# Two product blocks of the first weight tile inside the prologue of a one-core hybrid layer kernel

## What is computed

```python
h = rmsnorm(x, norm_mix_g)
proj = h @ w_in            # w_in: 1024 x 9232, f32
q, k, v, gate_a = slices of proj, 64 columns per head
k, v                       # also outputs (new_k, new_v)
```

## Time and profile before

| | |
|---|---|
| median of 3 runs | 2689.96 us (2687.56 to 2692.24) |
| span of the profiled execution | 2689.6 us |
| PE busy | 2613.3 us, 97% of the span |
| DVE, ACT, POOL busy | 1493.0, 876.8, 345.1 us |
| DMA moved | 214.21 MB, 80 GB/s on average |
| first 40th of the span (67 us) | PE busy 6 tenths, PE clock 8 tenths |
| every other 40th | PE busy 9 tenths but in three of them (7, 8, 7) |

### The profile page before, as it was taken

How to read it: one execution, slowest core, us unless ns; L and a number is a source line. 1 busy time by engine, 2 the same in 40 slices (tenths; PEclk the granted TensorE clock), 3 DMA queues, 4 the chain that set the end, 5 groups by cost and what they waited for, 6 DMA issues and landing times. The chain is left out here.

```text
span 2689.6 us, 47862 instructions
## 1 busy us (share of the span) xinstructions
PE 2613.3 (97%) x17088; PEld 2490.4 (93%) x17088; DVE 1493.0 (56%) x2513; ACT 876.8 (33%) x1708; POOL 345.1 (13%) x327
## 2 busy tenths in 40 slices
PE   6999999999999999999979999999999999999897
PEld 6888888888879999999979999999999999999897
DVE  4666766766675666666643443545444444444754
ACT  4433444434342636363631122211111111111513
POOL 0222322322231111111100002000000000000300
PEclk8999999999999999999979999999999999999999
DMA  7544544435645242424155433411111111111112
GB/s 135 90 107 81 100 100 93 101 79 108 75 75 67 30 103 32 100 33 101 32 202 186 162 102 125 145 40 47 39 39 47 39 45 40 39 47 39 36 41 81
DMA packets 331843, 214.21 MB, mean 80 GB/s; under 512 B 117828, under 2 KB 312216, under 8 KB 331672
## 3 DMA queue, kind: packets, MB, share of 16 engines
q1 hardware_dynamic: 331672, 211.98, 34.3%
HBM read 164.51 MB, written 47.41 MB: 79 GB/s over the span
## 5 line engine op out<-in xcount | busy, mean ns | idle before, releaser
L165 PE MATMUL bank<-operand_hi,w_hi 128*128 128x384 f32 x1584 | 532.9, 336 | 1.5 <-DVE w_lo L148 1.5
L165 PE MATMUL bank<-operand_hi,w_lo 128*128 128x384 f32 x1584 | 530.0, 335 | 0.0
L165 PE MATMUL bank<-operand_lo,w_hi 128*128 128x384 f32 x1584 | 529.9, 335 | 0.0
L139 ACT ACTIVATE w_hi<-w_raw 128x1024 fp32r<-128x1024 f32 (+1 forms) x167 | 172.7, 1034 | 782.0 <-PE bank L165 486.9
L165 PEld LDWEIGHTS bank<-operand_hi,w_hi 128*128 128x128 f32 x1584 | 297.5, 188 | 2.1 <-issue 1.8
L165 PEld LDWEIGHTS bank<-operand_lo,w_hi 128*128 128x128 f32 x1584 | 297.5, 188 | 0.3
L165 PEld LDWEIGHTS bank<-operand_hi,w_lo 128*128 128x128 f32 x1584 | 297.4, 188 | 0.0
L694 PE MATMUL acc<-operand_hi,w_hi 128*128 128x384 f32 x792 | 281.9, 356 | 6.4 <-PEq L215 6.4
L1153 POOL TENSOR_TENSOR wgt<-wgt,left 128x128 f32<-128x128 f32 (+2 forms) x224 | 210.1, 944 | 588.2 <-DVE left L1105 423.1
L694 PE MATMUL acc<-operand_hi,w_lo 128*128 128x384 f32 x792 | 267.8, 338 | 0.0
L694 PE MATMUL acc<-operand_lo,w_hi 128*128 128x384 f32 x792 | 267.2, 337 | 0.0
(11 more groups left out here) (356 smaller groups left out, 4457.8 us busy)
## 6 DMA issues: line engine op xcount, KB each, us to landing
w_raw<-in_w_in SPq DMA_DIRECT2D x65, 512.0 KB, 8.7
k_cache<-in_cache_k SPq DMA_DIRECT2D x256, 64.0 KB, 2.5
v_cache<-in_cache_v SPq DMA_DIRECT2D x64, 256.0 KB, 4.4
w_raw<-in_w_gate SPq DMA_DIRECT2D x22, 512.0 KB, 3.9
w_raw<-in_w_up SPq DMA_DIRECT2D x22, 512.0 KB, 3.8
w_raw<-in_w_down SPq DMA_DIRECT2D x22, 512.0 KB, 3.6
s_gate_a<-gate SPq DMA_DIRECT2D x24, 192.0 KB, 2.8
s_o<-o_t SPq DMA_DIRECT2D x8, 576.0 KB, 10.8
```

What stands on the lines that cost most here:

```text
L139: act.activation(hi, S.raw[u0 % 2][:, 0:cols], ACT.Copy).then_inc(S.hi_done, 1)
L165: last = pe.matmul(acc[:, 0:RBN], w[:, k, :], a[:, k, rows], start=(n == 0), stop=(n == 3 * kts - 1 and more is None))
```

## The change

PSUM banks `acc0` and `acc1` are opened before the prologue and passed on (`S.acc`), the table's own PSUM bank is dropped and the table turned into `pt[0]`. Product blocks 0 and 1 (48 matmuls, `first_product`) are issued inside the prologue: block 0 in three pieces behind the transposes of row tiles 6, 7 and 8, block 1 in two pieces around the table. In the pair stage `product` runs only for m >= 2. On SP weight tile 0 is loaded behind row tile 4, tile 1 behind row tile 8, tile 2 last; tile 3 is loaded at the start of the pair stage. ACT splits tile 0 behind the high part of row tile 3, DVE behind the low part of row tile 3. The low part of tile 1 and the two channel copies move from the prologue's end to the pair stage's start on DVE.

```diff
+def first_product(S, pe, acc, slot, rb, k0, k1):
+    hi, lo = [w[slot][:, :].rearrange("p (k c) -> p k c", k=KT) for w in (S.w_hi, S.w_lo)]
+    for k in range(k0, k1):
+        for n, (w, x) in enumerate(((hi, S.R0_hi), (hi, S.R0_lo), (lo, S.R0_hi))):
+            last = pe.matmul(acc[:, 0:RBN], w[:, k, :], x[:, k, rb * RBN:(rb + 1) * RBN],
+                             start=(k == 0 and n == 0), stop=(k == KT - 1 and n == 2))
+    if k1 == KT:
+        last.then_inc(S.acc_done, 1)
...
 def stage_prologue(nc, S, A, first_tiles):
...
-                for r in range(2, RT):
+                for r in range(2, 5):
                     rows_in(r)
+                S.W.load(sp, 0, 2, 0, first_tiles[0])
+                for r in range(5, RT):
+                    rows_in(r)
+                S.W.load(sp, 1, 2, 0, first_tiles[1])
...
-                S.W.load(sp, 0, 2, 0, first_tiles[0])
-                S.W.load(sp, 1, 2, 0, first_tiles[1])
                 S.W.load(sp, 2, 2, 0, first_tiles[2])
-                S.W.load(sp, 3, 2, 0, first_tiles[3])
...
                 for r in range(3, RT):
                     high(r)
-                S.W.split_hi(act, 0, 2, 0, HEAD)
+                    if r == 3:
+                        S.W.split_hi(act, 0, 2, 0, HEAD)
                 S.W.split_hi(act, 1, 2, 0, HEAD)
...
                         if r >= 2:
                             low(r - 2)
+                        if r == 5:
+                            S.W.split_lo(dve, 0, 2, 0, HEAD)
                 low(RT - 2)
                 low(RT - 1)
-                S.W.split_lo(dve, 0, 2, 0, HEAD)
-                S.W.split_lo(dve, 1, 2, 0, HEAD)
...
+                def first_block(m, k0, k1):
+                    pe.wait_ge(lo_ev, 3 * m + 3)
+                    pe.wait_ge(S.lo_done, HEAD + 1)
+                    first_product(S, pe, acc[m], 0, m, k0, k1)
+
                 for r in range(RT):
...
                     last.then_inc(x_t, 1)
+                    if r >= 6:
+                        first_block(0, 3 * (r - 6), min(3 * (r - 5), KT))
+                first_block(1, 0, 4)
                 pe.wait_ge(vec_in, 6 * 16)
-                pe.transpose(pv[:, :], vec_rows[:, :], S.ident[0:V_ALL, 0:V_ALL]).then_inc(vec_t, 1)
+                pe.wait_ge(lo_ev, RT - 2)
+                pe.transpose(pt[0][:, 0, 0:V_ALL], vec_rows[:, :], S.ident[0:V_ALL, 0:V_ALL]).then_inc(vec_t, 1)
+                first_block(1, 4, KT)
...
 def stage_pairs(nc, S, A, b0, u0, tiles, next_tiles, fourth_tile):
...
+            S.W.load(sp, u0 + 3, 2, 0, fourth_tile)
             for b in range(4):
                 cache_k(0, b)
...
             for m in range(PRE_BLOCKS):
-                pe.wait_ge(S.lo_done, HEAD + u0 + m // 3 + 1)
-                pe.wait_ge(S.acc_read_a, HEAD + b0 + m - 1)
-                product(b0 + m, m // 3, m, 0, KT)
+                if m >= 2:
+                    pe.wait_ge(S.lo_done, HEAD + u0 + m // 3 + 1)
+                    pe.wait_ge(S.acc_read_a, HEAD + b0 + m - 1)
+                    product(b0 + m, m // 3, m, 0, KT)
...
+            S.W.split_lo(dve, u0 + 1, 2, 0, HEAD)
+            dve.wait_ge(S.par_in, 48)
+            for h in range(2):
+                dve.tensor_copy(S.d_chan[64 * h:64 * h + 64, :],
+                                S.d_heads[64 * h:64 * h + 64, :].rearrange("p (k h) -> p k h", h=2)[:, :, h])
             for m in range(PRE_BLOCKS):
```

More of the change, by code:

```diff
@@ L203, in stage_prologue @@
         mask_g = sb("mask_g", [P, 64])
+        acc = S.acc
         pt = [ctx.enter_context(nc.psum_tensor(f"x_t{n}", [P, KT, P], F32)) for n in range(3)]
-        pv = ctx.enter_context(nc.psum_tensor("vec_t", [P, V_ALL], F32))
         vec_in, par_in, gain_in = sem("vec_in"), sem("par_in"), sem("gain_in")
         x_in = [sem(f"x_in{n}") for n in range(RT)]
+        S.par_in = par_in
         made, sq_done, root_done, h_done = sem("made"), sem("sq_done"), sem("root_done"), sem("h_rows_done")
@@ L352, in _ @@
                             low(r - 2)
+                        if r == 5:
+                            S.W.split_lo(dve, 0, 2, 0, HEAD)
                 low(RT - 2)
                 low(RT - 1)
-                S.W.split_lo(dve, 0, 2, 0, HEAD)
-                S.W.split_lo(dve, 1, 2, 0, HEAD)
                 dve.wait_ge(vec_t, 1)
[L358 to L363, removed]
+                dve.tensor_copy(S.vec[:, :], pt[0][:, 0, 0:V_ALL])
             @block.tensor
@@ L521, in unit, with stage_pairs @@
         return HEAD + NU * self.i + u + 1
-def stage_pairs(nc, S, A, b0, u0, tiles, next_tiles):
+def stage_pairs(nc, S, A, b0, u0, tiles, next_tiles, fourth_tile):
     N = NH // 2
@@ L558, in bank @@
             return ctx.enter_context(nc.psum_tensor(name, [P, 512], F32))
-        acc = [bank("acc0"), bank("acc1")]
+        acc = S.acc
         zb = [bank("z0"), bank("z1")]
@@ L2820, in four @@
             return [t(0, 0), t(0, 1), t(1, 0), t(1, 1)]
+        early = ExitStack()
+        S.acc = [early.enter_context(nc.psum_tensor(f"acc{n}", [P, 512], F32)) for n in range(2)]
         with ExitStack() as tmp:
@@ L2832, in hybrid_step @@
             S.dt_t = S.v_rows[0][:, :, :].rearrange("p r c -> p (r c)")
-            pairs_part = stage_pairs(nc, S, A, b, u, pair_tiles, [dt_tile, pair_tiles(NH // 2 - 1, 2)] + ssd_first)
+            pairs_part = stage_pairs(nc, S, A, b, u, pair_tiles, [dt_tile, pair_tiles(NH // 2 - 1, 2)] + ssd_first, first[3])
             u, b, ba, t0 = 4 * NH // 2 + 1, (4 * NH // 2 + 1) * NRB, (4 * NH // 2 + 1) * NRB, TP_PAIRS
+        early.close()
         S.o_in = [sem(f"o_in{n}") for n in range(4)]
```

## The result

The changed kernel took **2697.73 us** (median of 12 runs, 2693.77 to 2705.61). The kernel before, run beside it, took 2690.82 us (12 runs, 2684.29 to 2699.83). The ratio is 1.0024, 95% interval [1.0014, 1.0035]: slower by a quarter of a percent, 6.9 us between the medians. The profiled execution of the changed kernel is the slowest of its 12, at 2705.61 us, so lengths of its whole span say less than positions in its first 200 us, where it can be compared step by step.

The account below looks back on a forecast made before the run. PE, busy in 97% of the span, bounds the kernel, with the store chain behind the prologue tight. Span 2689.6 + 7.5 (block 2's lateness contained in it) = 2697.1, plus 0.4 to the median: 2697.5 us; range 2689.3 to 2702.0.

Parts of the forecast that it names:

- Step 1: Prologue: tile 0 ahead of row tiles 5 to 8 takes 9.2 us, making row tile 5's square 8.2 us late.
- Rival (b): Prologue rows aren't held up: tile 0 in front costs row tile 5 only 1.3 us; 2689.6 us; 10%.
- Step 2: Prologue: with 48 matmuls in it, PE ends at 50.6 us, later than DVE, and sets the barrier.
- Step 3: Behind the barrier: block 2 starts at 52.3 us instead of 50.31, +2.0 us.
- Step 4: SP behind the barrier: tile 3 issued at 52.7 us, first store at 65.6 us, +7.5 us.
- Who pays: Turn 0: stores and later loads on SP run 7.5 us late, and PE stands 7.5 us later near 133 us.
- (a): Store chain has room: drains and stores recover before 133 us, leaving only block 2's +2.0 us; 2692.0 us; 13%.
- (c): Rows not held up and store chain has 5.5 us room at 133 us: -5.9 us, 2684.1 us; 6%.
- (d): PE's clock stays low through the prologue: PE ends at 57.9 us, another 7.3 us late; 2704.8 us; 6%.

Follow-up runs that it names:

- e4: The kernel before with only weight tile 0 loaded behind row tile 4, in front of row tiles 5 to 8: 2699.05 us, ratio 1.0034.
- e2: The changed kernel with weight tile 3 loaded behind the 16 key-cache loads instead of in front of them: 2697.12 us, ratio 1.0024.
- e1: The changed kernel with weight tile 0 loaded behind row tile 8 again: 2691.13 us, ratio 1.0002 to the kernel before.
- e5: e1 with the stores of the first three k blocks issued ahead of the 16 key-cache loads: 2694.2 us, ratio 1.0015.
- e3: The changed kernel with tile 0 behind row tile 8 and tile 3 behind the key-cache loads: 2692.24 us, ratio 1.0010.
- e8: e5 with tile 0's split put later, where the tile has landed: 2690.81 us, ratio 1.0000 to the kernel before.
- e6: The kernel before with only the stores of the first three k blocks issued ahead of the key-cache loads: 2696.51 us, ratio 1.0020.

## Why the prediction was right, and where its steps were not

The forecast was 2697.5 us and slower; 2697.73 was measured. By its steps:

- **Step 1, the rows behind tile 0: right, a little small.** Row tile 5 at 22.8 was predicted, 24.1 measured (4.26 + 19.8), its square at 24.04 instead of 22.8. The factors came at 30.46 (30.0 predicted). Tile 0 took nearer the upper end of 10.5 than the 9.2 taken. Rival (b) is excluded: 49 GB/s with the weight tile in flight, 390 as soon as it had landed, and e4 shows the cost alone, 8.4 us at block 2. The line rate that the Trainium skill states for pieces of 512 B or more (DMA: Bandwidth & Descriptors, Specifications) isn't what these 512 B pieces got.
- **Step 2, the matmuls in the prologue: right.** Transposes of row tile 6 at 36.71 (36.4 predicted), last matmul ending at 50.4 (50.6). The clock rose between the transposes of row tile 6 (1.97 us for eight, at 36.71) and those of row tile 8 (1.04 us, at 44.00): the eight of row tile 7 at 41.36 took 1.22 us, 3 us behind the first product matmul at 38.34. The forecast had the rise at 36.4 + 5.5 = 41.9; counted from the first matmul it would have been 43.8. That the rows' lateness is nearly hidden by the 48 matmuls is confirmed by the pair e4 and the change: block 2 at 58.68 without them, at 51.91 with them.
- **Step 3, block 2: right**, 51.91 against 52.3, +1.6 instead of +2.0.
- **Step 4, the first store: mis-sized.** Tile 3 was issued at 52.24 (52.7 predicted). The term "tile 4, alone, landed after 9.0 us" was taken for it; it measured 11.6, with the cache loads issued in the same time. With 4.5 us behind it in place of 3.9 the first store came at 68.37, +10.3 and not +7.5, still inside the step's ends.
- **The reason given in step 4 was only half of it.** The text followed the issue of the first store. e2 moved that issue forward by 9.5 us and left the ratio at 1.0024. What reaches PE is the landing: DVE refills one of two `kv_out` buffers only when its last store has landed, and stores land behind the weight tiles ahead of them in the one queue.
- **Who pays: the place was right, the price too low.** PE was to show waits of several us between 75 and 140 us for DVE or ACT; it showed 2.04 us at 71.93 and 2.46 at 119.84. "PE stands at that place 7.5 us later" (133.66): measured 144.54, +10.9. The first wait also lies ahead of the forecast's 75 to 140 us. The 2.8 us of the first store and the low clock behind the waits, which had no term, are in it. The medians ended 6.9 us apart, below the 10.9 of the profiled turn 0; that the forecast hits to 0.2 us is owed to these two deviations cancelling. What gives the 4 us back behind turn 0 stays open: part shows by the last `s_o` store (8.8 us late), and the rest is within what single executions differ by.
- **Rivals.** (a), room in the store chain, is refuted by the growth from +1.6 at block 2 to +10.9. (c) and (d) did not happen; e1 shows that (c) would have failed even with the rows on time, since its lead of 4.2 us was given back at the stores.

## What to carry to other kernels

A DMA queue that is served in order is a schedule: a slow transfer (here a weight tile of 9 to 12 us against 1.3 us for a row tile of equal size) delays everything behind it, so write down who stands behind it and when each is wanted before moving it. Work that is moved forward by a few us pays only if the next shared chain, here store, landing, buffer free, moves too; check that chain in the trace before counting the gain, and look at landings, not at issues. Where the issuing engine waits for data, put other issues there: weaving the same list brought the changed kernel from 1.0024 to 1.0005 (two chip jobs, and the intervals touch) and, with tile 0 behind the rows and its split late, to 0.9981.

## What the runs showed that I had not expected

- **A short PE wait can cost twice.** In the changed kernel a wait of 2.04 us was followed by a granted clock of 0.79 from 72 to 80 us, which cost 1.8 us more, and one of 2.46 us by 0.83 from 120 to 140, which cost 3.6. Not every wait does it: e5 had 0.74 from 113.5 to 120 us behind its wait of 3.35 us, but 1.00 from 84 to 100 behind the one of 3.04 us at 84.20, and e2 had 1.00 from 116 to 136 behind 2.15 us at 115.89. What tells them apart I did not settle.
- **Issuing a DMA can block the engine for microseconds.** 16 key-cache loads were issued in 8.1 to 8.3 us where no weight tile was in flight (e2, e3, e5 to e8), in 14.5 to 19.6 us behind one or more (e1, the change, the kernel before, e4), with nothing else to wait for.
- **Making stores earlier can make a kernel slower.** In e6 the kernel before lost 0.20% [0.11, 0.29] to an order that issues its first stores 6 us sooner; tile 4 and the v stores went out 6 us later by it.
